# Inverting the triangular blocks from the transposed inverse, with the triangle itself as stationary operand

## What is computed

```
kbeta = kc * beta
l_mat = where(strict, (kbeta @ kc.T) * decay, 0)
a_mat = eye + l_mat
sol   = triangular_solve(a_mat, [v * beta, kbeta * exp(gcum)], lower, unit_diagonal)
```

## Time and profile before

| | |
|---|---|
| runs, median (lowest to highest) | 1303.62 us (1303.28 to 1305.38), 3 runs |
| the profiled execution, its own time | 1303.67 us |
| its span in the profile | 1301.4 us |
| PE busy over the span | 1255.1 us, 96% |
| DVE, ACT busy | 696.9 us (54%), 410.7 us (32%) |
| one step of the mixer's loop | about 35.5 us |

### The profile page before, as it was taken

How to read it: one execution, slowest core, us unless ns; L and a number is a source line. 1 busy time by engine, 2 the same in 40 slices (tenths; PEclk the granted TensorE clock), 3 DMA queues, 4 the chain that set the end, 5 groups by cost and what they waited for, 6 DMA issues and landing times.

```text
span 1301.4 us, 17346 instructions
## 1 busy us (share of the span) xinstructions
PE 1255.1 (96%) x6360; PEld 1062.5 (82%) x6360; DVE 696.9 (54%) x1069; ACT 410.7 (32%) x754; POOL 148.3 (11%) x183
## 2 busy tenths in 40 slices
PE   6999999997999999899999999999999999999997
PEld 5888888876888889778888888888888888888875
DVE  6332454657767777563563636363636363535366
ACT  5121243645444444353312121212121212121321
POOL 1321001302322232121000000000000000000005
PEclk9999999997999999999999999999999999999999
DMA  8321233564233331232211111111111111110133
GB/s 275 123 80 54 81 103 103 150 190 121 73 110 109 108 108 45 92 106 81 78 52 46 50 44 53 41 55 39 58 36 60 34 62 34 62 34 30 37 125 129
DMA packets 90762, 106.52 MB, mean 82 GB/s; under 512 B 17471, under 2 KB 75615, under 8 KB 90719
## 3 DMA queue, kind: packets, MB, share of 16 engines
q1 hardware_dynamic: 90719, 105.96, 25.2%
HBM read 82.84 MB, written 23.10 MB: 81 GB/s over the span
## 4 chain that ended last, share of the span: by engine, by line
PE 53%; POOL 1%; issue 1%; DVE 0%; ACT 0%; POOLq 0%; DVEq 0%
PE f_ps_up L2383 12%; PE f_ps_up L2385 12%; PE f_ps_up L2384 12%; PE sums L2394 5%; PE sums L2395 5%; PE sums L2396 5%; POOL stage L2101 1%; POOL f_conv L2101 0%; POOL f_stat L2367 0%; POOLq L2006 0%; DVE split L2336 0%; DVE h_t L2301 0%; DVE f_conv L2101 0%; ACT x_tile L2233 0%; DVE h_t L2259 0%
## 5 line engine op out<-in xcount | busy, mean ns | idle before, releaser
L2383 PE MATMUL f_ps_up<-split,f_w_hi 128*128 128x512 f32 x704 | 274.3, 390 | 1.7 <-DVEq L2237 1.5
L2385 PE MATMUL f_ps_up<-split,f_w_lo 128*128 128x512 f32 x704 | 273.9, 389 | 0.0
L2384 PE MATMUL f_ps_up<-split,f_w_hi 128*128 128x512 f32 x704 | 273.9, 389 | 0.0
L2247 DVE SCALAR_TENSOR_TENSOR f_conv<-f_ps_up,f_taps,f_conv 128x1023 f32<-128x1023 f32 x88 | 112.8, 1282 | 272.3 <-ACT f_conv L2176 266.8
L2383 PEld LDWEIGHTS f_ps_up<-split,f_w_hi 128*128 128x128 f32 x704 | 132.1, 188 | 29.9 <-DVEq L2237 1.9
L2385 PEld LDWEIGHTS f_ps_up<-split,f_w_lo 128*128 128x128 f32 x704 | 132.1, 188 | 27.5
L2176 ACT ACTIVATE f_conv<-f_ps_up,f_taps 128x1024 f32<-128x1024 f32 x44 | 53.1, 1207 | 321.4 <-PE f_ps_up L2385 321.4
L2384 PEld LDWEIGHTS f_ps_up<-split,f_w_hi 128*128 128x128 f32 x704 | 132.2, 188 | 27.3
L2259 DVE TENSOR_TENSOR h_t<-sums,h_t 128x512 f32<-128x512 f32 x168 | 111.0, 685 | 39.9 <-PE sums L2396 39.7
L2394 PE MATMUL sums<-f_w_hi,f_y_hi 128*128 128x512 f32 x320 | 124.6, 389 | 0.0
L2396 PE MATMUL sums<-f_w_hi,y_lo 128*128 128x512 f32 x320 | 124.5, 389 | 0.0
(11 more groups left out here) (320 smaller groups left out, 2058.8 us busy)
## 6 DMA issues: line engine op xcount, KB each, us to landing
stage<-in_w_up SPq DMA_DIRECT2D x22, 1024.0 KB, 5.1
stage<-in_w_down SPq DMA_DIRECT2D x11, 1024.0 KB, 4.9
x_tile<-in_x SPq DMA_DIRECT2D x12, 512.0 KB, 4.0
stage<-in_w_in SPq DMA_DIRECT2D x6, 1024.0 KB, 6.7
qkv<-conv SPq DMA_DIRECT2D x11, 512.0 KB, 3.6
rows<-p_row SPq DMA_DIRECT2D x8, 644.0 KB, 3.2
stage<-rows SPq DMA_DIRECT2D x8, 644.0 KB, 4.0
res<-x_tile SPq DMA_DIRECT2D x8, 512.0 KB, 2.9
```

The costliest lines, as they stand in the source:

```text
L2247: op = dve.scalar_tensor_tensor(conv[:, q, k:S], ps_up[:, q % 2, 0:S - k], taps[:, bass.ds(ct + (FTAPS - 1 - k) * 2 * FT, 1)], conv[:, q, ...
L2383: pe.matmul(bank, hi, h_hi[:, k, cols], start=(k == ends[0]), stop=False)
L2384: pe.matmul(bank, hi, h_lo[:, k, cols], start=False, stop=False)
L2385: op = pe.matmul(bank, lo, h_hi[:, k, cols], start=False, stop=(k == ends[1]))
```

## The change

The levels are worked on the transposed side. With `low` as the stationary operand and `inv_t` as the moving one, `a_off` gives the transpose of X L directly; it is masked with the mirrored block masks (the same table columns, other contents), multiplied with `inv` as stationary operand, and added to `inv_t` at all three levels. `a_trinv` now turns `inv_t`, and `a_turn` copies to `inv`. The four transposes of `a_trl` and the copy `a_lowt` are gone for every tile. Since `low` is now read until the last level of the next step, it has two buffers in place of `low` and `low_t`, chosen by the parity of the tile. Waits change with it: `a_off(4)` waits for the load of `inv_t` where it waited for the load of `inv`, and `a_inv(4)` the other way round; `a_low` has one wait more, for `a_off(6)` two tiles back; `a_norms` waits for `a_bv` two tiles back in place of `a_lowt`. Shapes and counts of everything that stays are the same.

```diff
-        t[:, T_LEVEL + n * P:T_LEVEL + (n + 1) * P] = (i // (2 * s) == j // (2 * s)) & ((i // s) % 2 == 1) & ((j // s) % 2 == 0)
+        t[:, T_LEVEL + n * P:T_LEVEL + (n + 1) * P] = (i // (2 * s) == j // (2 * s)) & ((i // s) % 2 == 0) & ((j // s) % 2 == 1)
...
-        low = sb("low", [P, H, P])
-        low_t = sb("low_t", [P, H, P])
+        low = sb("low", [P, 2, H, P])
...
-            def a_lowt(u):
-                after(act, front, u, F_TRL)
-                act.copy(low_t[:], bank("a1")).then_inc(lowt_set.sem, 1)
-
             def a_turn(t, n):
                 after(act, level, t, L_TR[n])
-                act.copy(inv_t[:], bank("a1")).then_inc(turned.sem, 1)
+                act.copy(inv[:], bank("a1")).then_inc(turned.sem, 1)
...
                 after(dve, low_out, u - 1)
+                after(dve, level, u - 2, L_OFF[6])
                 after(dve, front, u, F_KK)
                 for h in range(H):
-                    op = dve.scalar_tensor_tensor(low[:, h], bank("a0")[:, h], k_gate[:, par, K_LOW, h:h + 1], dec[:, h], ALU.mult, ALU.mult)
+                    op = dve.scalar_tensor_tensor(low[:, par, h], bank("a0")[:, h], k_gate[:, par, K_LOW, h:h + 1], dec[:, h], ALU.mult, ALU.mult)
...
-                m, which = (inv, 0) if n < LV else (inv_t, 1)
-                dve.tensor_tensor(halves(m[:], n, which), ps_half(n, which), halves(m[:], n, which), ALU.add).then_inc(added.sem, 1)
+                dve.tensor_tensor(halves(inv_t[:], n, 1), ps_half(n, 1), halves(inv_t[:], n, 1), ALU.add).then_inc(added.sem, 1)
...
-                after(pe, lowt_set, u - (not (isinstance(u, int) and u == 0)))
+                if isinstance(u, int) and u == 0:
+                    after(pe, dec_set, 0, 2)
+                else:
+                    after(pe, bv_set, u - 2)
...
-            def a_trl(u):
-                after(pe, low_set, u)
-                after(pe, dec_set, u, 2)
-                after(pe, bv_set, u - 1)
-                for h in range(H):
-                    op = pe.transpose(bank("a1")[:, h], low[:, h], ident)
-                op.then_inc(front.sem, 1)
-
-            def a_off(t, n, a):
+            def a_off(t, par, n, a):
                 if n == FIRST:
-                    after(pe, inv_in, t)
-                    after(pe, lowt_set, t)
+                    after(pe, inv_t_in, t)
+                    after(pe, low_set, t)
...
-                    op = pe.matmul(bank("a0")[:, h], low_t[:, h], inv[:, h], start=True, stop=True)
+                    op = pe.matmul(bank("a0")[:, h], low[:, par, h], inv_t[:, h], start=True, stop=True)
...
                 if n == FIRST:
-                    after(pe, inv_t_in, t)
+                    after(pe, inv_in, t)
...
-                    if n < LV:
-                        op = pe.matmul(ps_half(n, 0)[:, h], inv_t[:, h], half_cols(off[:], h, n, 0), start=True, stop=True)
-                    else:
-                        op = pe.matmul(ps_half(n, 1)[:, h], off[:, h], half_cols(inv_t[:], h, n, 1), start=True, stop=True)
+                    op = pe.matmul(ps_half(n, 1)[:, h], inv[:, h], half_cols(off[:], h, n, 1), start=True, stop=True)
...
-                    op = pe.transpose(bank("a1")[:, h], inv[:, h], ident)
+                    op = pe.transpose(bank("a1")[:, h], inv_t[:, h], ident)
```

More of the change, by code:

```diff
@@ L775, in mix_block @@
         E_KTR, E_NORM = 1, 2
-        front = tally("front", 5)
-        F_DEC, F_DECT, F_KK, F_TRL, F_KQ = range(1, 6)
+        front = tally("front", 4)
+        F_DEC, F_DECT, F_KK, F_KQ = range(1, 5)
         vtr = tally("vtr")
@@ L792, in mix_block @@
         q_n2, k_n2, k_sq, rn, gate_set = tally("q_n2"), tally("k_n2"), tally("k_sq"), tally("rn", 2), tally("gate_set", 2)
-        dec_set, kout_set, low_set, lowt_set = tally("dec_set", 2), tally("kout_set"), tally("low_set"), tally("lowt_set")
+        dec_set, kout_set, low_set = tally("dec_set", 2), tally("kout_set"), tally("low_set")
         qk_set, bv_set = tally("qk_set"), tally("bv_set")
@@ L920, in _, with store_low @@
             blocks_of = lambda m: m[:, 0:BASE * BASE].rearrange("g (r c) -> g r c", c=BASE)
-            def store_low(u):
+            def store_low(u, par):
                 ready((low_set, u, 1), (blk_in, u - 1, 16))
-                sp.dma_start(whole(scratch["low"]), low[:]).then_inc(low_out.sem, 16)
+                sp.dma_start(whole(scratch["low"]), low[:, par]).then_inc(low_out.sem, 16)
             def load_blk(u):
@@ L978, in _ @@
             load_first(0, H, s_first_q)
-            store_low(0)
+            store_low(0, 0)
             load_blk(0)
@@ L1005, in step @@
                 if a:
-                    store_low(t + 1)
+                    store_low(t + 1, 1 - par)
                 if not d:
@@ L1282, in _ @@
             conv_silu(act, kept, 4, 0)
-            a_lowt(0)
             c_exp(0, 0)
@@ L1319, in step @@
                     c_exp(t + 1, 0)
-                    a_lowt(t + 1)
                     c_pt(t + 1, 0)
@@ L1760, in a_trinv @@
                 elif n == FIRST:
-                    after(pe, lowt_set, t)
+                    after(pe, q_n2, t)
                 else:
@@ L1910, in _ @@
             multiply(pe, kept, 4, 1, 0, A1)
-            a_trl(0)
             c_scores(0, 0, 0)
@@ L1937, in step @@
                     b_ks(t, par)
-                B(a_off, 4, a)
+                B(a_off, par, 4, a)
                 A(a_decay, F_DEC)
@@ L1945, in step @@
                 B(a_trinv, 4, a)
-                B(a_off, 5, a)
+                B(a_off, par, 5, a)
                 A(c_trk)
@@ L1956, in step @@
                 B(a_vtr, par)
-                B(a_off, 6, a)
+                B(a_off, par, 6, a)
                 D_(d_mm, 0, [0, 1])
                 B(a_inv, 6)
-                A(a_trl)
                 A(c_trp, 0)
```

## The result

The changed kernel takes 1306.95 us (median of 20 runs, 1304.90 to 1309.81), the kernel before 1304.45 us in the same session (20 runs, 1301.87 to 1308.98). The ratio is 1.0019, with a 95% interval of 1.0012 to 1.0026: slower by 2.5 us. The forecast of 1303.6 us and its range up to 1305.4 us missed it. The profiled execution took 1306.78 us with a span of 1304.6 us, 3.2 us more than the span before.

What follows compares the result with a forecast made beforehand. The prediction took the loop to be bound by PE up to `a_inv(6)`, then DVE's chain with ACT at its end. Transposes gained 0.05 us, all else 0: 1303.67 - 0.05 = 1303.6 us, range 1302.0 to 1305.4.

Steps and rivals of the forecast that it cites:

- the ring: In the loop, PE from `c_trp` to `a_inv(6)`, then DVE and ACT to the next `c_trp`, set the time.
- the new wait at `b_vnew`: PE would newly wait for `a_add(6)` before `b_vnew`, 0.3 to 0.4 us in the steps that had none.
- the late waits of steps 2 to 6: PE's waits for ACT before the second `c_trp` of a step; forecast about 0.1 us longer.
- the 0.34 of the working: Step 2: of the 0.45 us of removed transposes, 0.34 becomes a new wait at `b_vnew`.
- the check list: Signs in the later profile: no transposes of `low`, `b_vnew` wait 0.3 to 0.4 us, loop step still 35.5 us.
- copy: ACT's removed copy between its two `c_exp`, 8 x 0.585 = 4.7 us of ACT; claimed gain 0.
- swapped loads: `a_off(4)` now waits for `inv_t`, which SP issues last; 3.6 us of slack in the tightest case, so 0.
- the wait of `a_low`: Added wait before DVE's `a_low`, met two tiles earlier; cost taken as 0, upper bound 0.9 us.
- rival A: PE is the bound and all removed transposes count, 8 x 0.45 = 3.6 us: 1300.0 us, 0.3% faster; chance 0.11.
- the sum: Whole kernel: 1303.67 - 0.05 = 1303.6 us, the 0.05 from step 1's transposes, every other term 0.
- Every one has ACT behind it, so there the gain is 0: PE's seven waits before the second `c_trp` (prologue, step 0, steps 2 to 6) end with ACT; removing transposes gains 0.
- Rival B: PE's clock falls in one stretch each of steps 2 to 6: 1310.8 us, slower by 0.55%; chance 0.04.

Runs made afterwards that it cites:

- e5: Kernel before with 18 empty semaphore instructions on PE ahead of the first `c_trp`; 1305.21 us, ratio 0.9999 to the kernel before.
- e12: Kernel before with 18 do-nothing instructions (waits that hold at once) at the start of PE's program; 1306.58 us, ratio 1.0011 to the kernel before.
- e2: Changed kernel with 18 empty semaphore instructions on PE in the prologue, ahead of the first `c_trp`; 1306.63 us, ratio 1.0008 to the kernel before.
- e8: Changed kernel with ACT's copy of `low` kept, unread, `a_off(4)` waiting for it, no transposes on PE; 1306.75 us, ratio 1.0014 to the kernel before.
- e7: Changed kernel with the old transposes on PE, ACT's copy (unread) and the waits on it put back; 1303.96 us, ratio 0.9993 to the kernel before.
- e3: Changed kernel with step 0's load of `w_out` row block 7 issued behind the load of the blocks; 1307.08 us, ratio 1.0016 to the kernel before.

## Why the prediction was wrong

**Right: the ring.** "So from the end of `a_inv(6)` to `c_trp` two ways run side by side". A step is 35.5 us as before; the new wait at `b_vnew` came, the late waits of steps 2 to 6 grew by 0.05 to 0.18, about the 0.1 of the forecast (step 2 has 1.03 against 0.96), and nothing was gained in the loop. The delay at `b_vnew` is the 0.34 of the working: it starts 370.28 - 369.51 = 0.77 us behind `c_trp`, where it was 0.43. The row shows only 0.17 of it as idle, because it counts from the end of `c_trp` and not from where the next product could have been issued; the check list should have said 0.17.

**Right: copy, swapped loads, the wait of `a_low`, each at 0.** DVE's wait for `a_kk` before `a_low` is 4.0 us in 7 times in both kernels. No load of the halves of the inverse shows up as a releaser.

**Right: the doubt about rival A.** PE was not the bound, and 1300.0 us did not come.

**Wrong: the sum, and with it the range.** "Against the profiled execution: 1303.67 - 0.05". The step that failed is step 0's part of it. "Every one has ACT behind it, so there the gain is 0" is right as far as it goes: the wait of 7.39 us before the late `c_trp` of step 0 covers what PE does. But the sum also took the moment at which this wait ends as fixed, and in the profiled execution it ended 3.14 us later. The releaser of that wait is ACT, ACT's is DVE, and DVE had already waited 1.13 us for the blocks from memory in step 0: on that chain a late transfer is paid in full. The sum has a term for each instruction that goes or waits, and none for what the missing instructions do to the moments of PE's own instruction fetches; in the profiled execution that term was about 1.6 us (1.44 in e5). It was priced at nothing without being looked at: the DMA view has the row "q8 instruction" in the kernel before too (26 packets over the span), and the prediction read the DMA queues only for `inv_t`. The other 1.56 us are the clock's.

**The clock: not excluded, not settled.** Rival B looked for it in steps 2 to 6, where it stayed full in every run. The range held "one stretch of low clock around steps 0 and 1 more or less", but as scatter around an unchanged middle, and "the trace has no drop from gaps of this size" looked away from steps 0 and 1: in the kernel before the clock fell at 320.1 us, after an idle time of 1.65 us, and in the changed one at 281.6, after 1.95. In step 0 one stretch more at 1.2 GHz costs the profiled execution 1.56 us, close to the 1.4 of that sentence. It appears in 7 of the 14 profiles: in 6 of the 9 kernels with the changed levels, and in e12 alone of the 5 with the old ones. It is missing from e2 and e8, where PE has the changed kernel's work. So it comes without the change and need not come with it; whether the change makes it more frequent is open. Of the changed kernel's 20 executions 13 have a mean granted clock of 0.990 or less, of the 99 of the kernel before 46. These numbers are too few to show it. The changed kernel's 20 have a mean span of 1304.4 us at a mean clock of 0.9898, the 99 one of 1302.8 at 0.9907: of these 1.6 us 0.7 are left at equal clock, and the rest goes with the clock. (Beside the changed kernel the kernel before took 1304.45 us, in the later sessions 1304.65 to 1305.13.) Why the clock was lower, by the change or by chance in one session, stays open, and with it how the 2.5 us divide.

## What to carry to other kernels

Where a kernel changes by one part in a thousand, look at the transfers on the critical chain before counting instructions: list where the instruction fetches lie (the DMA view by short windows has them) and ask which of them stands within two microseconds of a transfer that an engine waits for. An edit that only removes work moves these fetches, and a pad, or useless work kept, can hide or bring back as much as the edit was to gain; so test an edit against a copy with the removed work left in and unused, as e7 does, before calling it good or bad. Compare executions with the same mean granted clock as well as the medians: here a mean clock of 0.990 in place of 0.992 went with 2.6 us, as much as the whole effect. And a long wait before an instruction is a cover only for the side that waits.

## What the runs showed of the hardware

- Instructions come over the same DMA engines as data, in packets of 16 KB (and some of 8 KB). One took 0.88 to 2.06 us in the 14 profiles. Where it fell among the packets of a 256 KB store, 20 to 32 of the store's 512 packets began late, and the store landed after 3.8 to 4.4 us in place of 2.3 to 2.5. In the kernel before, from the fetch at 133.2 to the one at 337.2, the trace has 1008 products, 1009 weight loads and 66 other instructions on PE, 2083 in the eight intervals, or 260 for each fetch. Single intervals hold between 142 and 396. The Trainium skill (Runtime: NRT & Kernel Launch, Instruction fetch mechanics) has the refill in blocks of 256 instructions, 16 KiB; by that, this trace agrees on average. It calls the cost of such a crossing "mostly hidden". For PE it was: in the kernel before and the changed one, PE's idle times from 292 to 312 us all end with an instruction of DVE or ACT. For a transfer of another engine it was not: 1.0 to 1.6 us at the late `c_trp` here.
- The fetch's moment is repeatable (297.0 and 297.2 in two kernels with the same program on PE, 292.4 and 291.6 in the changed kernel and e3) and yet jumps: 18 instructions brought it from 297.0 to 289.9, and putting back the copy on ACT from 291.6 to 297.2.
- Instructions that do nothing cost time on PE: with 38 semaphore increments ahead of it `a_inv(4)` came after 3.06 us without a product in place of 1.95, and 96 instructions of waits that held at once moved PE's first product by 3.3 us beyond an idle start of 7.95 us.
